# Two layers of a decoder on one core: weight rounding moved among the last queries, and the order of the last head's vector work changed

## The chip, the cores and the metric

The kernel runs on one core of a Trainium2 chip. Its time is the device time of one execution, in microseconds (us). The engines are TensorE (PE, matrix products; its weight loads are listed apart as PEld), VectorE (DVE), ScalarE (ACT), GpSimd (POOL) and SyncE (SP), which issues the transfers from memory. Each engine runs its own list of instructions strictly in the order in which it was written, and waits for the others by semaphores.

## The reference, cut to what matters

The program computes four transformer-like layers for one sequence of 512 positions and width 1024 in float32: retention, latent attention, a short convolution mixer with its feed-forward layer, and differential attention with a second feed-forward layer. The change touches only the differential attention:

```python
k, v = shared_kv(x, g_kv, w_kv)
def diff_attention(h, k, v, dist_bias, w_q, lam_vecs, subln_g, w_o, lambda_init):
    q = (h @ w_q).reshape(b, nb, Q_BLOCK, N_HEADS, 2, HEAD_DIM).transpose(1, 0, 2, 3, 4, 5)
    lam = jnp.exp(jnp.sum(lv[0] * lv[1])) - jnp.exp(jnp.sum(lv[2] * lv[3])) + lambda_init
    def block(args):
        ...
        logits = jnp.einsum('bqhmd,bkhmd->bhmqk', qb.astype(jnp.float32), kf) * scale
        logits = logits + bias[None, :, None]
        ...
        probs = jax.nn.softmax(logits, axis=-1)
        attn = probs[:, :, 0] - lam * probs[:, :, 1]
        return jnp.einsum('bhqk,bkhe->bqhe', attn, vf)
    ...
    o = rms_norm(o, subln_g) * (1.0 - lambda_init)
    return o.reshape(b, s, V_WIDTH).astype(h.dtype) @ w_o
```

There are 8 heads. Each has two maps of scores (p = 0 and 1), which are softmaxed apart and then combined with the factor lambda. Queries come in four groups of 128 rows, i = 0 to 3; group i needs keys 0 to 128(i+1) only.

## The kernel before, in words

**Numbers in two parts.** Every float32 product is made of three products of rounded numbers (high by high, high by low, low by high). So each tensor that PE reads exists as a high part, rounded by ACT, and a low part, the difference, made by DVE or POOL.

**Weights.** The weights stream through in units of 8 blocks of 128x128, 512 KB each, in exactly the order in which PE uses them. SP loads a unit into one of 3 places of `stage`; ACT rounds it into `WH` (L795, `hi_to`), DVE subtracts it into `WL` (L804, `lo_to`), both rings of 4 units. A call `hi_to(act, b)` or `lo_to(dve, b)` does all units up to the one of block b plus 2 (`AHEAD`) that have not been done. PE waits for `w_lo` of a unit before its first product. The units that matter here:

- 209 and 210: queries of heads 6 and 7; 211: keys of head 0; 212 and 213: values of heads 0 and 1, the first and the second four steps of the sum; 214 and 215: keys of heads 1 and 2.
- 227: steps (0, 0) to (5, 0), (0, 1) and (0, 2) of the output projection, in the order of the table below; 228, 229 and 230 are the next ones.

```python
DIF_OUT = {
    "head 7, a": [(0, 0), (1, 0)],
    ...
    "head 7, c": [(4, 0)],
    "head 7, d": [(5, 0)],
    "turn": [(k, m) for k in range(2) for m in (1, 2, 3)],
    "values": [(k, m) for k in (2, 3, 4) for m in (1, 2, 3)],
```

**Start of the attention.** PE makes query(6), query(7), key(0) and the first half of value(0). Behind it DVE scales each query (L2920), ACT rounds it (L2791) and POOL makes its low part (L3102). A key goes the same way: DVE L2930, ACT L2804, POOL L3089. Only after POOL has made the low part of key 0 can PE begin the scores of head 0 (L2675). The order of this work on each engine is the order in which `act_dif`, `dve_dif`, `pool_dif` and `pe_dif` are written.

**A head.** For each group of rows PE makes both maps of scores (L2675) into two of three PSUM banks that are used in turn; DVE adds the bias and takes the maximum (L2949, listed as ISA or CUSTOM_DVE, which frees the bank); ACT takes the exponential (L2816). Then DVE combines the two maps of two groups at a time, `combine(h, 0)` for groups 0 and 1 and `combine(h, 2)` for groups 2 and 3: a reciprocal (L2959), the weight (L2963), two sums (L2969). PE transposes (L2688), ACT (L2823) and DVE (L2975) split the result (`turn`), PE multiplies by the values (`values`), and ACT squares (L2831). PE sums the squares (L2710, `sums_of`) into a bank of the three; DVE reads it (L2988) and takes the root in seven small instructions (L948 to L960); PE spreads it (L2720), ACT copies (L2839), DVE multiplies (L3001, `finish`), ACT and POOL split (L2844, L3095, `rounded`). `sums_of`, `finish` and `rounded` of head h run during heads h+1 and h+2.

**The last head.** Instead of a next key and value, PE has pieces of the output projection between the groups: a, scores of group 1, finish(5), b, scores of group 2, c, scores of group 3, values(6), d (which needs `rounded(5)`), turn of groups 0 and 1, sums_of(6), then the 6 steps "turn". Of these, the products for column 2 go into the bank that sums_of(6) used, so PE waits there until DVE has read the sums (L2988).

Of the kernel before, what the change touches and what calls it, by code (L numbers as in the profile page):

```python
# [15 lines left out]
KD = 8  # L16
# [229 lines left out]
BLOCK = {b: i for i, b in enumerate(ORDER) if b is not None}  # L246
# [64 lines left out]
class Net:  # L311
# [2470 lines left out]
    def act_dif(self, act):  # L2782
        QZ = self.dif_qz

        def key_input(k):
            act.activation(self.dif_xkv(0, k), self.xt(k), ACT.Copy, scale=self.col("g_kv_2", k)).then_inc(
                *self.tick("xg_hi", ("xkv_hi", k)))

        def query(h):
            act.wait_ge(*self.at("q_in", h))  # L2790
            act.activation(QZ[:, 1024 * h:1024 * h + 512], self.place["t", "dif", "q", h], ACT.Copy).then_inc(  # L2791
                *self.tick("q_hi", ("q_hi", h)))

        def key(h):
            if h >= 3:
                rounded(h - 3)
            if h % 2 == 0:
                self.hi_to(act, BLOCK["w_kv_2", KD - 1, h])
                if h:
                    self.hi_to(act, BLOCK["w_kv_2", 3, 9 + h])  # L2800
            act.wait_ge(*self.at("dif_kin", h))
            if h >= 2:
                act.wait_ge(*self.at("pe", "dif", "s", h - 2, 3, 1))
            act.activation(self.dif_k[h % 2][:, 0:512], self.place["t", "dif", "k", h], ACT.Copy).then_inc(  # L2804
                *self.tick("k_hi", ("k_hi", h)))
# [20 lines left out]
        def values(h):  # L2826
            t = ("t", "dif", "osq", "h", h)
            act.wait_ge(*self.at("pe", "dif", "pv", h))
            for w in self.freed(*t):
                act.wait_ge(*w)  # L2830
            act.activation(self.place[t], self.place["dif", "pv", h], ACT.Square).then_inc(  # L2831
                *self.tick("o_sq", ("o_sq", h)))
# [14 lines left out]
        def out(steps):  # L2847
            self.hi_to(act, BLOCK["w_o_2", steps[-1][0], steps[-1][1]])
# [9 lines left out]
        for k in range(4, KD):  # L2858
            key_input(k)
        query(6)  # L2860
        query(7)
        key(0)
        self.hi_to(act, BLOCK["w_kv_2", KD - 1, 9])
        value(0, [0])
        for h in range(8):
            scores(h, 0)
            if h:
                turn(h - 1, 3)
            scores(h, 1)
            if h >= 2:  # L2870
                finish(h - 2)
            scores(h, 2)
            if h < 7:
                key(h + 1)
            else:
                out(DIF_OUT["head 7, c"])
                rounded(5)
            scores(h, 3)
            if h:
                values(h - 1)  # L2880
            if h < 7:
                c = (h + 1) // 2
                turn(h, 0)
                turn(h, 1)
                value(c, [(h + 1) % 2])
                turn(h, 2)
                self.hi_to(act, BLOCK["w_kv_2", KD - 1, 9 + 2 * c if h % 2 else h + 1])
            else:
                out(DIF_OUT["turn"])
                turn(h, 0)  # L2890
                turn(h, 1)
# [13 lines left out]
    def dve_dif(self, dve):  # L2905
# [8 lines left out]
        def query(h):  # L2914
            t, b = ("t", "dif", "q", h), ("dif", "w", h) if h < 6 else ("dif", "q", h)
            dve.wait_ge(*self.at("pe", *b))
            dve.wait_ge(*self.at("r", "dif", "pre"))
            for w in self.freed(*t):
                dve.wait_ge(*w)
            dve.tensor_tensor(self.place[t], self.place[b], R, ALU.mult).then_inc(  # L2920
                *self.tick("q_in", ("q_in", h), ("free", *b)))

        def key(h):
            if h % 2 == 0:
                self.lo_to(dve, BLOCK["w_kv_2", KD - 1, h])
            t, b = ("t", "dif", "k", h), ("dif", "k", h)
            dve.wait_ge(*self.at("pe", *b))
            for w in self.freed(*t):
                dve.wait_ge(*w)
            dve.tensor_tensor(self.place[t], self.place[b], R, ALU.mult).then_inc(  # L2930
                *self.tick("dif_kin", ("dif_kin", h), ("free", *b)))
# [4 lines left out]
        def scores(h, i):  # L2936
            n = 128 * (i + 1)
            if i == 0:
                for p in range(2):
                    self.small(("ds", h, p), 4)  # L2940
                dve.wait_ge(*self.at("bias_table"))
            mx = self.small(("dmx", h, i), 2)
            for p in range(2):
                b = ("dif", "s", h, i, p)
                dve.wait_ge(*self.at("pe", *b))
                if p == 0 or i >= 2:
                    for w in self.freed(*self.dif_row(h, i, p)):
                        dve.wait_ge(*w)
                dve.tensor_tensor_reduce(self.dif_s(h, i, p), self.place[b][:, 0:n], TB[:, h, 512 - n:512], -0.125,  # L2949
                                         3.0e38, ALU.add, ALU.min, mx[:, p:p + 1]).then_inc(  # L2950
                    *self.tick("biased", ("biased", h, i, p), ("free", *b)))

        def combine(h, a):


            w, pair = self.small(("dw", h), 4), slice(a, a + 2)
            s0, s1 = [self.small(("ds", h, p), 4) for p in range(2)]
            dve.wait_ge(*self.at("exp", "dif", h, a + 1, 1))
            dve.reciprocal(w[:, pair], s1[:, pair]).then_inc(*self.tick("row_rec", ("row_rec", "dif", h, a)))  # L2959
            dve.wait_ge(*self.at("row_rec", "dif", h, a))  # L2960
            if (h, a) == (0, 0):
                dve.wait_ge(*self.at("lam"))
            dve.scalar_tensor_tensor(out=w[:, pair], in0=s0[:, pair], scalar=self.lam, in1=w[:, pair], op0=ALU.mult,  # L2963
                                     op1=ALU.mult).then_inc(*self.tick("row_rec", ("weight", h, a)))
            dve.wait_ge(*self.at("weight", h, a))
            for i in (a, a + 1):
                t0, t1 = [self.dif_s(h, i, p) for p in range(2)]
                done = [("free", *self.dif_row(h, i, 1))] if i >= 2 else []
                dve.scalar_tensor_tensor(out=t0, in0=t1, scalar=w[:, i:i + 1], in1=t0, op0=ALU.mult,  # L2969
                                         op1=ALU.add).then_inc(*self.tick("probs", ("probs", "dif", h, i), *done))  # L2970
# [23 lines left out]
        def finish(h):  # L2994
            t, b = ("t", "dif", "t", h), ("dif", "pv", h)
            dve.wait_ge(*self.at("head_r", h))
            if h == 0:
                dve.wait_ge(*self.at("sub_gain"))
            for w in self.freed(*t):
                dve.wait_ge(*w)  # L3000
            dve.scalar_tensor_tensor(out=self.place[t], in0=self.place[b], scalar=self.gs,  # L3001
                                     in1=self.place["t", "dif", "r", h], op0=ALU.mult, op1=ALU.mult).then_inc(
                *self.tick("head_out", ("head_out", h), ("free", *b)))

        def out(steps):
            self.lo_to(dve, BLOCK["w_o_2", steps[-1][0], steps[-1][1]])
# [23 lines left out]
        for k in range(4, KD):  # L3030
            key_input(k)
        query(6)
        query(7)
        key(0)
        self.lo_to(dve, BLOCK["w_kv_2", KD - 1, 9])
        value(0, [0])
        for h in range(8):
            scores(h, 0)
            if h >= 2:
                sums_of(h - 2)  # L3040
            if h:
                turn(h - 1, 3)
            if h % 2:
                self.lo_to(dve, BLOCK["w_kv_2", KD - 1, h])
            scores(h, 1)
            combine(h, 0)
            if h >= 2:
                finish(h - 2)
            scores(h, 2)
            if h < 7:  # L3050
                key(h + 1)
            else:
                out(DIF_OUT["head 7, c"])
            scores(h, 3)
            c = (h + 1) // 2
            if h % 2 and h < 7:
                self.lo_to(dve, BLOCK["w_kv_2", 3, 9 + 2 * c])
            combine(h, 2)
            floor_of(h)
            if h < 7:  # L3060
                turn(h, 0)
                turn(h, 1)
                value(c, [(h + 1) % 2])
                turn(h, 2)
                if h % 2:
                    self.lo_to(dve, BLOCK["w_kv_2", KD - 1, 9 + 2 * c])
            else:
                out(DIF_OUT["turn"])
                turn(h, 0)
                turn(h, 1)  # L3070
# [300 lines left out]
```

## Time and profile before

| What | us |
|---|---|
| Median of 3 runs | 2036.31 |
| Lowest and highest of them | 2034.36, 2037.73 |
| The profiled execution's own time | 2038.49 |
| Span of the profiled execution | 2036.70 |
| PE busy in that span | 1973.4 |
| DVE, ACT, POOL busy | 1253.0, 833.8, 320.7 |
| Mean granted clock of PE, share of full | 0.986 |

A kernel in which PE is busy 97% of the span loses time only where PE stands still, or where its clock is granted at half. All times below are from the start of the span. The differential attention lasts from about 1349 to 1599 us, its last head from 1525 to 1561 us.

### The profile page before, as it was taken

To read this page: it belongs to the slowest core of one execution; us is meant where nothing else is said; L and a number is where in the kernel's file an instruction comes from. 1 tells how busy PE (TensorE), PEld (TensorE's weight loads), DVE (VectorE), ACT (ScalarE), POOL (GpSimd) and SP (SyncE) were. 2 spreads that over 40 slices of the span, in tenths; PEclk is the share of its full clock that TensorE was granted. 3 is DMA by queue.
4 is the path that set the end of the run, shared out by engine and by line. 5 is a ranking of instruction groups with operands and counts; after the bars stand their busy time and mean duration, and the time that the engine had idled before them with its cause. 6 is when DMAs were issued, how large, how long until landed. Compare 5 with 4: busy or idle time off the path is not lost.

```text
span 2036.7 us, 27328 instructions
## 1 busy us (share of the span) xinstructions
PE 1973.4 (97%) x10578; PEld 1692.0 (83%) x10578; DVE 1253.0 (62%) x2219; ACT 833.8 (41%) x1389; POOL 320.7 (16%) x256
## 2 busy tenths in 40 slices
PE   7999999999889999999999999999999999999997
PEld 6889888887778887898888888988887988888896
DVE  6666666267555474457877623786763778775256
ACT  4333333244365443244444423554554444443243
POOL 3332242101132200110111110112111011110101
PEclk9999999999889999999999999999998999999998
DMA  4222222322111224232232422223112323233321
GB/s 156 99 82 88 94 78 73 104 83 95 63 32 32 85 94 129 79 103 93 93 103 85 128 88 93 84 86 112 55 42 63 93 83 99 89 112 114 97 71 62
DMA packets 54824, 179.03 MB, mean 88 GB/s; under 512 B 6279, under 2 KB 10887, under 8 KB 54696
## 3 DMA queue, kind: packets, MB, share of 16 engines
q1 hardware_dynamic: 54696, 177.29, 27.0%
q8 instruction: 84, 1.38, 0.3%
q14 instruction: 44, 0.36, 0.1%
HBM read 172.55 MB, written 4.72 MB: 87 GB/s over the span
## 4 chain that ended last, share of the span: by engine, by line
PE 66%; DVE 5%; ACT 2%; issue 2%; POOL 1%; DVEq 0%; ACTq 0%; POOLq 0%
PE pb L821 62%; DVE WL L804 1%; PE pb L2675 1%; PE pb L921 1%; ACT WH L795 1%; PE pb L2204 0%; PE pb L905 0%; DVE X L1002 0%; PE pb L1719 0%; DVE FD L993 0%; DVE T L2949 0%; PE pb L2720 0%; DVE FR L2910 0%; PE pb L909 0%; POOL FR L2115 0%
## 5 line engine op out<-in xcount | busy, mean ns | idle before, releaser
L821 PE MATMUL pb<-FR,WH 128*128 128x512 f32 (+1 forms) x5100 | 1455.3, 371 | 21.2 <-DVE WL L804 11.4
L821 PEld LDWEIGHTS pb<-FR,WH 128*128 128x128 f32 x5100 | 920.4, 190 | 183.0 <-DVE WL L804 11.4
L821 PE MATMUL pb<-FR,WL 128*128 128x512 f32 (+1 forms) x2550 | 939.6, 368 | 0.0
L804 DVE TENSOR_TENSOR WL<-stage,WH 128x1024 fp32r<-128x1024 f32 x311 | 402.1, 1310 | 407.0 <-ACT WH L795 405.8
L821 PEld LDWEIGHTS pb<-FR,WL 128*128 128x128 f32 x2550 | 484.2, 190 | 80.8
L795 ACT ACTIVATE WH<-stage 128x1024 fp32r<-128x1024 f32 x311 | 319.7, 1051 | 116.8 <-PE pb L821 107.3
L821 PE MATMUL pb<-WH,FR 128*128 128x256 f32 x832 | 156.4, 285 | 2.9 <-DVE T L1306 1.5
L821 PE MATMUL pb<-FR 128*128 128x256 f32 (+3 forms) x752 | 126.1, 319 | 14.0 <-POOL FR L2115 10.0
L821 PEld LDWEIGHTS pb<-FR 128*128 128x128 f32 x752 | 114.1, 198 | 28.4 <-POOL FR L2115 11.1
L821 PEld LDWEIGHTS pb<-WH,FR 128*128 128x128 f32 x832 | 132.0, 192 | 4.5 <-DVE WL L804 2.0
L1285 POOL TENSOR_TENSOR acc<-acc,T 128x512 f32<-128x512 f32 (+1 forms) x53 | 63.7, 1203 | 418.0 <-ACT T L1256 274.9
L821 PE MATMUL pb<-WL,FR 128*128 128x256 f32 x416 | 117.8, 283 | 0.0
L1012 ACT ACTIVATE FR<-X,cols 128x256 fp32r<-128x256 f32 (+1 forms) x88 | 52.2, 605 | 96.9 <-DVE X L1002 96.9
L2428 POOL TENSOR_TENSOR FR<-FD,FR 128x512 fp32r<-128x512 f32 x26 | 33.7, 1297 | 312.7 <-ACT FR L2358 312.7
L821 PEld LDWEIGHTS pb<-WL,FR 128*128 128x128 f32 x416 | 79.9, 192 | 0.1
L1256 ACT ACTIVATE T<-pb 128x512 f32<-128x512 f32 (+1 forms) x51 | 27.3, 535 | 106.0 <-PE pb L821 106.0
L2184 ACT ACTIVATE FD<-FD,cols 128x512 f32<-128x512 f32 x42 | 29.5, 721 | 81.4 <-DVE FD L2389 52.0
L1044 DVE SCALAR_TENSOR_TENSOR FR<-X,cols,FR 128x256 fp32r<-128x256 f32 (+1 forms) x88 | 52.6, 608 | 9.3 <-ACT FR L1012 9.2
L1610 POOL TENSOR_TENSOR FR<-T,FR 128x512 fp32r<-128x512 f32 (+3 forms) x32 | 31.1, 1003 | 158.5 <-ACT FR L1445 158.5
L993 DVE SCALAR_TENSOR_TENSOR T<-FD,cols,pb 128x256 f32<-128x256 f32 x112 | 50.2, 474 | 6.6 <-PE pb L921 6.6
L883 ACT ACTIVATE FR<-pb,held 128x256 fp32r<-128x256 f32 x64 | 26.9, 472 | 64.3 <-PE pb L821 64.0
L892 DVE SCALAR_TENSOR_TENSOR FR<-pb,held,FR 128x256 fp32r<-128x256 f32 x64 | 27.9, 478 | 35.1 <-ACT FR L883 34.9
(227 smaller groups left out, 1673.9 us busy)
## 6 DMA issues: line engine op xcount, KB each, us to landing
stage<-in_ws SPq DMA_DIRECT2D x311, 512.0 KB, 3.6
X<-in_xT SPq DMA_DIRECT2D x8, 256.0 KB, 5.8
FD<-in_decay SPq DMA_DIRECT2D x8, 256.0 KB, 3.8
FD<-scr SPq DMA_DIRECT2D x1, 2048.0 KB, 8.8
out_dram<-X SPq DMA_DIRECT2D x16, 128.0 KB, 1.7
scr<-FD SPq DMA_DIRECT2D x10, 160.0 KB, 5.3
FD<-in_rope_b SPq DMA_DIRECT2D x2, 512.0 KB, 3.5
FD<-in_pT SPq DMA_DIRECT2D x4, 256.0 KB, 5.3
```

What stands on the lines that cost most here:

```text
L795: act.activation(hi, src, ACT.Copy).then_inc(*self.tick("w_hi", ("w_hi", u)))
L804: dve.tensor_tensor(lo, src, hi.bitcast(F32), ALU.subtract).then_inc(*self.tick("w_lo", ("w_lo", u)))
L821: m = pe.matmul(out, l, r, start=first and i == 0, stop=last and i == n - 1)
L892: i = dve.scalar_tensor_tensor(out=lo, in0=src, scalar=self.hold(y)[:, t:t + 1], in1=hi.bitcast(F32), op0=ALU.mult, op1=ALU.subtract)
L993: dve.scalar_tensor_tensor(out=part(t, p), in0=part(self.Y[k], p), scalar=self.col(name, base + k), in1=part(self.place["spread", *key], p ...
L1012: act.activation(part(self.xin(at)(0, k), p), part(self.xt(k), p), ACT.Copy, scale=self.col(name, base + k)).then_inc(*self.tick("xg_hi", ...
L1044: dve.scalar_tensor_tensor(out=part(xin(1, k), p), in0=part(self.xt(k), p), scalar=self.col(name, base + k), in1=part(xin(0, k), p).bitcas ...
L1256: act.activation(part(self.place["t", s, "osq", m], p), b, ACT.Square).then_inc(*self.tick("osq", ("osq", s, m, *q)))
L1285: pool.tensor_tensor(acc, acc, part(self.place["t", s, "osq", m], p), ALU.add).then_inc(*self.tick("acc", *done))
L1610: pool.tensor_tensor(S[:, 1280 + o:1280 + o + n], self.place["t", "ret", "s", h, j][:, 0:n], S[:, o:o + n].bitcast(F32), ALU.subtract).the ...
L2184: act.activation(self.place[o], self.place[u], ACT.Copy, scale=w).then_inc(*self.tick("tap", done))
L2428: pool.tensor_tensor(self.ffn_in(s, 1, m), self.place[t], self.ffn_in(s, 0, m).bitcast(F32), ALU.subtract).then_inc(*self.tick("m_lo", ("f ...
```

## The change: what it does

No instruction is added or removed on any engine, and PE's, POOL's and SP's lists stay as they are. ACT's and DVE's are reordered in two places.

```diff
@@ act_dif
         query(6)
+        self.hi_to(act, BLOCK["w_kv_2", KD - 1, 0])
         query(7)
+        self.hi_to(act, BLOCK["w_kv_2", KD - 1, 9])
         key(0)
-        self.hi_to(act, BLOCK["w_kv_2", KD - 1, 9])
         value(0, [0])
...
             if h < 7:
                 key(h + 1)
             else:
-                out(DIF_OUT["head 7, c"])
                 rounded(5)
             scores(h, 3)
             if h:
                 values(h - 1)
+            if h == 7:
+                out(DIF_OUT["head 7, c"])
@@ dve_dif
         query(6)
+        self.lo_to(dve, BLOCK["w_kv_2", KD - 1, 0])
         query(7)
+        self.lo_to(dve, BLOCK["w_kv_2", KD - 1, 9])
         key(0)
-        self.lo_to(dve, BLOCK["w_kv_2", KD - 1, 9])
         value(0, [0])
...
             scores(h, 1)
-            combine(h, 0)
-            if h >= 2:
+            if h < 7:
+                combine(h, 0)
+                if h >= 2:
+                    finish(h - 2)
+                scores(h, 2)
+                key(h + 1)
+                scores(h, 3)
+            else:
+                scores(h, 2)
                 finish(h - 2)
-            scores(h, 2)
-            if h < 7:
-                key(h + 1)
-            else:
+                combine(h, 0)
+                scores(h, 3)
                 out(DIF_OUT["head 7, c"])
-            scores(h, 3)
```

The two engines' lists show it. In the queries, DVE before: FD<-pb,R are the queries 6 and 7, L804 the weight units, R<-pb,R is key 0, and the last row is the first half of the values.

```order
L2910 SCALAR_TENSOR_TENSOR FR<-X,cols,FR 128x512 x4
L2920 TENSOR_TENSOR FD<-pb,R 128x512 x2
L804 TENSOR_TENSOR WL<-stage,WH 128x1024
L2930 TENSOR_TENSOR R<-pb,R 128x512
L804 TENSOR_TENSOR WL<-stage,WH 128x1024 x2
L892 SCALAR_TENSOR_TENSOR FR<-pb,held,FR 128x256 x2
```

and DVE with the change, where each line from 2910 on has a number higher by 2:

```order
L2912 SCALAR_TENSOR_TENSOR FR<-X,cols,FR 128x512 x4
L2922 TENSOR_TENSOR FD<-pb,R 128x512
L804 TENSOR_TENSOR WL<-stage,WH 128x1024
L2922 TENSOR_TENSOR FD<-pb,R 128x512
L804 TENSOR_TENSOR WL<-stage,WH 128x1024 x2
L2932 TENSOR_TENSOR R<-pb,R 128x512
```

Unit 213 has moved ahead of query 7, and units 214 and 215 have moved ahead of key 0.

The same place on ACT, as a difference; L2791 rounds queries, L2804 key 0, L795 weight units, L883 the values.

```order
-L2791 ACTIVATE FR<-FD 128x512 x2
-L795 ACTIVATE WH<-stage 128x1024
+L2791 ACTIVATE FR<-FD 128x512
+L795 ACTIVATE WH<-stage 128x1024
+L2791 ACTIVATE FR<-FD 128x512
+L795 ACTIVATE WH<-stage 128x1024 x2
 L2804 ACTIVATE FR<-R 128x512
-L795 ACTIVATE WH<-stage 128x1024 x2
 L883 ACTIVATE FR<-pb,held 128x256 x2
```

ACT has moved in step with DVE: key 0 is now behind both later units here too.

In the last head, DVE before, from the scores of group 2 back to the combination of groups 0 and 1 (L2959 to L2969), with finish(5) at L3001, unit 229 at L804 and the scores of group 3 at 128x512:

```order
L2959 RECIPROCAL sm<-sm 128x2
L2963 SCALAR_TENSOR_TENSOR sm<-sm,keep 128x2
L2969 SCALAR_TENSOR_TENSOR T<-T,sm 128x128
L2969 SCALAR_TENSOR_TENSOR T<-T,sm 128x256
L3001 SCALAR_TENSOR_TENSOR acc<-pb,keep,R 128x512
L2949 ISA FD,sm<-pb,FD 128x384
L2949 ISA sm 128x1
L2949 ISA FD,sm<-pb,FD 128x384
L2949 ISA sm 128x1
L804 TENSOR_TENSOR WL<-stage,WH 128x1024
L2949 ISA T,sm<-pb,FD 128x512
```

and with the change:

```order
L2951 ISA FD,sm<-pb,FD 128x384
L2951 ISA sm 128x1
L2951 ISA FD,sm<-pb,FD 128x384
L2951 ISA sm 128x1
L3003 SCALAR_TENSOR_TENSOR acc<-pb,keep,R 128x512
L2961 RECIPROCAL sm<-sm 128x2
L2965 SCALAR_TENSOR_TENSOR sm<-sm,keep 128x2
L2971 SCALAR_TENSOR_TENSOR T<-T,sm 128x128
L2971 SCALAR_TENSOR_TENSOR T<-T,sm 128x256
L2951 ISA T,sm<-pb,FD 128x512
```

The scores of group 2 now come first, then finish(5), then the combination, and unit 229 follows the scores of group 3. On ACT unit 229 has moved from behind the exponentials of group 2 to behind the squares of head 6 (L2831), next to unit 230.

## Rows read from the trace of the kernel before

**Rows 1.** The page: busy time by engine, and the chain that ended last, by engine.

```profile
PE 1973.4 (97%) x10578; PEld 1692.0 (83%) x10578; DVE 1253.0 (62%) x2219; ACT 833.8 (41%) x1389; POOL 320.7 (16%) x256
...
PE 66%; DVE 5%; ACT 2%; issue 2%; POOL 1%; DVEq 0%; ACTq 0%; POOLq 0%
```

**Rows 2.** Chain of waits, 1380 to 1400 us: start, length, what.

```profile
1386.17 4.58 PE pb L821 x36
```

**Rows 3.** Timeline of PE: start, length, what, [idle before <- releaser].

```profile
1386.17 0.39 PE L821 MATMUL pb<-WH,FR 128*128 128x256 f32 x1 [1.05 <-DVE WL L804]
...
1390.68 0.55 PE L2675 MATMUL pb<-FR 64*128 64x128 f32 x6
```

**Rows 4.** Timeline of DVE, queries to values.

```profile
1383.99 2.13 DVE L804 TENSOR_TENSOR WL<-stage,WH 128x1024 fp32r<-128x1024 f32 x1 [1.65 <-ACT WH L795]
1386.04 0.68 DVE L2930 TENSOR_TENSOR R<-pb,R 128x512 f32<-128x512 f32 x1
1388.37 2.61 DVE L804 TENSOR_TENSOR WL<-stage,WH 128x1024 fp32r<-128x1024 f32 x2 [1.65 <-ACT WH L795]
```

**Rows 5.** Timeline of ACT, same stretch.

```profile
1381.78 1.23 ACT L2791 ACTIVATE FR<-FD 128x512 fp32r<-128x512 f32 x2 [5.25 <-DVE FD L2920]
1382.91 1.05 ACT L795 ACTIVATE WH<-stage 128x1024 fp32r<-128x1024 f32 x1
...
1387.29 1.99 ACT L795 ACTIVATE WH<-stage 128x1024 fp32r<-128x1024 f32 x2
```

**Rows 6.** Timeline of POOL, same stretch.

```profile
1382.49 2.55 POOL L3102 TENSOR_TENSOR FR<-FD,FR 128x512 fp32r<-128x512 f32 x2 [3.21 <-ACT FR L2791]
1387.46 1.29 POOL L3089 TENSOR_TENSOR FR<-R,FR 128x512 fp32r<-128x512 f32 x1 [2.43 <-ACT FR L2804]
```

**Rows 7.** Timeline of PE, last head.

```profile
1515.76 2.12 PE L821 MATMUL pb<-FR 128*128 128x512 f32 x12
...
1530.66 0.79 PE L2675 MATMUL pb<-FR 64*128 64x384 f32 x6
...
1534.25 0.97 PE L2675 MATMUL pb<-FR 64*128 64x512 f32 x6 [1.91 <-DVE sm L2949]
1535.15 3.65 PE L821 MATMUL pb<-FR 128*128 128x512 f32 x12
...
1541.44 1.45 PE L2710 MATMUL pb<-ones,T 128*128 128x1 f32 x8 [0.82 <-ACT T L2831]
```

**Rows 8.** Chain of waits, last head.

```profile
1544.54 5.66 PE pb L821 x15
...
1562.05 3.57 PE pb L821 x15
```

**Rows 9.** Timeline of DVE, last head.

```profile
1531.77 0.17 DVE L2959 RECIPROCAL sm<-sm 128x2 f32<-128x2 f32 x1 [1.16 <-ACT T L2816]
...
1532.89 0.74 DVE L3001 SCALAR_TENSOR_TENSOR acc<-pb,keep,R 128x512 f32<-128x512 f32 x1
1533.55 0.54 DVE L2949 CUSTOM_DVE_ANT_0 FD<-pb,FD 128x384 f32<-128x384 f32 x1
...
1536.90 1.23 DVE L804 TENSOR_TENSOR WL<-stage,WH 128x1024 fp32r<-128x1024 f32 x1 [2.32 <-ACT WH L795]
...
1540.94 0.17 DVE L2959 RECIPROCAL sm<-sm 128x2 f32<-128x2 f32 x1 [1.59 <-ACT T L2816]
...
1542.67 1.22 DVE L804 TENSOR_TENSOR WL<-stage,WH 128x1024 fp32r<-128x1024 f32 x1
```

**Rows 10.** Timeline of ACT, last head.

```profile
1539.39 0.72 ACT L2816 ACTIVATE T<-T,sm 128x512 f32<-128x512 f32 x1 [1.99 <-DVE sm L2949]
...
1540.81 0.57 ACT L2831 ACTIVATE T<-pb 128x512 f32<-128x512 f32 x1
```

**Rows 11.** Stretches: us, busy (count) of PE, PEld, DVE, ACT, POOL; granted clock; DMA.

```profile
1384.00:1386.00 2.00, 1.13 (x10) 0.92 (x8) 2.00 (x1) 0.00 (x0) 1.03 (x1) 1.00 0.52 200
...
1546.00:1548.00 2.00, 2.00 (x6) 1.61 (x5) 0.00 (x0) 0.00 (x0) 0.00 (x0) 0.50 0.36 145
```

## Prediction

> **What bounds the kernel now.** I first read the busy times and the chain that ended last. PE is busy for 1973.4 of 2036.70 us, and the chain runs through PE for two thirds of the span [rows 1]. The change gives PE no work and takes none away, so only PE's standing time and its clock can change. The largest possible gain is what PE loses at the two places.
>
> The first place is in the queries. In the timeline of PE the reader is to see one stop: at 1386.17 the second half of value(0) had waited 1.05 us for the low part of unit 213, so PE wanted it at 1385.12. The scores of head 0 follow at 1390.68, without a stop [rows 3]. In the chain of waits PE's 36 products lead up to them, to 1386.17 + 4.58 = 1390.75 [rows 2]: key 0 was ready before. How long before: DVE scales key 0 at 1386.04 [rows 4], and POOL's low part ends at 1387.46 + 1.29 = 1388.75 [rows 6]. That is 2.71 us for the key's way through DVE, ACT and POOL, and it leaves a slack of 1390.68 - 1388.75 = 1.93 us. This slack is what the change draws on.
>
> The second place is the last head. PE stops three times: 1.91 us for a bank that DVE frees with the scores of group 2, 0.82 us for ACT's squares [rows 7], and, in the chain, the restart at 1544.54 for column 2 of the steps "turn" [rows 8], where it has waited for DVE to read the sums of head 6.
>
> **The change, first place.** ACT rounds queries 6 and 7 in 1382.91 - 1381.78 = 1.13 us from start to start, 0.57 each, and then unit 213; DVE starts on that 1383.99 - 1382.91 = 1.08 us later [rows 4, 5]. With unit 213 behind query 6 alone, ACT starts it at 1382.34 and DVE at 1383.42. DVE's subtraction of a unit takes 1.22 us where POOL is idle [rows 9]. Here it took 2.13 [rows 4], beside POOL's two query parts, which ran to 1382.49 + 2.55 = 1385.04 [rows 6]. POOL will by then have only the part of query 6, to about 1383.77, so I charge 0.35 us of standing still: the low part is ready at 1383.42 + 1.22 + 0.35 = 1385.0. PE wants it at 1385.12. The stop of 1.05 us goes, and value(0) ends at 1390.68 - 1.05 = 1389.63.
>
> But key 0 now comes after units 214 and 215. Step by step: DVE scales query 7 from 1385.0 to 1385.6 (0.6, as key 0 of the same size, 0.68 with its overlap [rows 4]); ACT rounds it to 1386.2; ACT rounds unit 214 to about 1387.25, half of its pair of 1.99 plus the handover [rows 5], and unit 215 a microsecond later, ahead of DVE. The slot of unit 215 is free, since PE is through with key 0 before value(0). DVE subtracts both in 2.61 [rows 4], from 1387.25 to 1389.8, again with some 0.3 us beside POOL (now query 7's part, then key 0's). Then key 0 needs its 2.71: 1392.5. PE, which could have gone on at 1389.63, stands for 2.9 us, and the scores of head 0 start 1392.5 - 1390.68 = 1.8 us later than now. All that is queued behind them on PE (key 1, the other groups, the second half of value 0) comes later by as much; DVE and ACT wait for those scores in turn, so nothing ahead of them can catch up. Bounds: if POOL does not hold up DVE and key 0 follows at once, 1.3; if DVE is held up through both units, at the pace of unit 213, 2.61 becomes up to 4.3, and the loss 3.5, but that needs POOL to be busy all the while, and it has one part of 1.3 us to do. I take 1.8 and 1.3 to 2.3.
>
> The Trainium skill, "SBUF — State Buffer", section "Who interferes with whom", says that a DVE instruction with two SBUF inputs and a GpSimd instruction that reads SBUF exclude each other, and that the first to start has the port for its whole length. By that rule unit 213 in the changed kernel waits for the end of query 6's part and then takes 1.22, the same 1385.0; were the rule untrue, it would be ready at 1384.65, which changes nothing, since PE does not want it sooner.
>
> **The clock behind the new stop.** In the last head a stop of 1.91 us was followed by twelve products of values(6) in 3.65 us, where those of values(5) took 2.12 [rows 7]: 1.5 us lost. The stop of 1.05 us in the queries left the granted clock at 1.00 [rows 11]. The new stop of 2.9 us is longer than the one that cost 1.5, so I take 1.5 for it. Behind it, PE is the engine that the chain follows [rows 2], so the loss is on the path. Bounds: nothing if the clock stays, and 2.1, which is what fifteen products lost at half clock, 5.66 against 3.57 us [rows 8]. The two levels here are 2.4 and 1.2 GHz: a stretch inside those fifteen shows 0.50 [rows 11].
>
> **The change, second place.** PE's scores of group 2 start at 1530.66 [rows 7] and DVE can read them some 0.8 us later, at 1531.5, when they are written (0.79). It reads them now only at 1533.55, behind the combination and finish(5) [rows 9]. Moved ahead, both maps are done at about 1532.5 and the first bank is free at 1532.0 (0.54 us for a map, and they overlap a little [rows 9]). PE's stop of 1.91 us goes: it starts group 3 at 1534.25 - 1.91 = 1532.34.
>
> That is not yet a gain at the end, since PE meets DVE again at the restart of 1544.54. DVE goes on: finish(5) 1532.5 to 1533.15 (0.66, from 1532.89 to 1533.55), the combination to 1534.3 (1.12, from 1531.77 to 1532.89), and the scores of group 3 to 1535.5 (1.2 for two of 128x512). ACT takes the exponentials to 1536.95 (1540.81 - 1539.39 = 1.42) and the squares of head 6 to 1537.45 [rows 9, 10]. Only then does it round unit 229, for 1.04, and DVE, which had to wait 2.32 us for this unit before [rows 9], waits again, now until 1538.5. It subtracts to 1539.65, and the second combination follows at once; it started at 1540.94 before [rows 9]. So it is 1.3 us earlier, not 1.9: the unit that moved behind the squares on ACT has taken the rest. From the combination to PE's restart 1544.54 - 1540.94 = 3.6 us go by, all on DVE (the combination, unit 230, two turns, the reading of the sums), and none of it changes. PE restarts at 1543.25: 1.3 us of gain. Bounds: 0.6, if ACT's squares or unit 229 come later than I have them, and 1.9, the whole stop.
>
> PE will have done its earlier pieces sooner and then stands for some 4 us ahead of that restart. It now loses 2.1 us there to the half clock [rows 8]; it will do so again. I take no difference, with 1.3 either way.
>
> **The sum.** 1.8 + 1.5 - 1.3 = +2.0 us, against the profiled execution's own 2038.49 (its span of 2036.70 and 1.79 around it), that is 2040.5. This execution was 2.18 above the median of the runs, 2036.31; against the median the sum gives 2038.3.
>
> **Rivals.**
> - *No clock loss behind the first stop.* What speaks for it: the clock was kept over 1.05 us [rows 11]. Against it: the longer stop. The sum is +0.5: 2036.8. The Trainium skill, "TensorE: Matmul & The Clock Gate", section "What's actually happening", says that the intervals in which the chip watches PE run freely and are not tied to the kernel's start. By that rule the same stop costs more or less from one execution to the next; no rows of one execution can show this.
> - *The half clock lasts: slower.* If it holds behind the new stop for twice as long as it did over values(6), it costs 2 x 1.5 = 3.0 [rows 7], and with 1.8 and -1.3 the sum is +3.5: 2039.8. From a clock term of 4.07 - 0.5 = 3.6 us on, the change is slower by more than 0.2%: 2040.4 and more. For it: the new stop is the longest in this part, and head 0 at half pace may make new stops, each of which feeds the next. Against it: 3.6 us is more than any row shows; the longest, over fifteen products, is 2.1 [rows 8].
> - *The gain side.* The key's delay does not reach PE (DVE would have to be done with both units by 1387 instead of 1389.8), so that the first place gives its 1.05, and the second gives 1.3 and keeps its full clock, another 2.1: -4.45, 2031.9. Against it: [rows 4] have the duration of the pair, and a stop of 4 us stands ahead of that restart.
> - *The last head gives nothing.* PE only moves its waiting, and DVE's wait for unit 229 grows by as much as the scores were advanced: 0 there, +3.3 in all: 2039.6.
>
> **How the numbers follow.** 0.2% is 4.07 us, about what a measurement can tell from no change. My forecast, +1 to +3, has 0.46; without clock loss, -1 to +1, 0.22; the last head without gain, 0.14, all three within 0.2%, as are half of the lasting half clock (0.12 in all) and some of the gain side (0.06). This makes 0.86 within, 0.09 slower and 0.05 faster. The range for 8 in 10 reaches from -1.5 (both places with their good bounds, no clock loss) to +4.3: 2034.8 to 2040.6.
>
> **What would show it.** In the changed profile: PE runs through unit 213 near 1385 without a stop; a new stop of 2.5 to 3.3 us ahead of the scores of head 0, ended by POOL's L3096 (the key's low part, L3089 now); the granted clock at 0.5 for a stretch behind it; DVE's L804 twice ahead of L2932. In the last head, counted from its first scores: no stop ahead of the scores of group 3, a stop of about 4 us ahead of column 2 that DVE ends, and DVE's wait for unit 229 ahead of the second combination. I am wrong if DVE subtracts units 214 and 215 much faster than in 2.61, if PE's delay at head 0 is taken up by slack in head 0, or if the half clock falls elsewhere than where I have it.

## The result, and the profile after

| | before | changed |
|---|---|---|
| Median of 10 executions each, us | 2036.97 | 2042.62 |
| Lowest and highest | 2034.36, 2039.80 | 2039.54, 2044.93 |
| Span of the profiled execution | 2036.70 | 2043.1 |
| Mean granted clock of PE in it | 0.986 | 0.985 |

The ratio is 1.0023, with an interval of 1.0015 to 1.0031. The changed kernel is slower, by 5.65 us between the medians. The forecast was 2038.3 with a range of 2034.8 to 2040.6: the result lies outside, on the side of slower. Two executions of this study, one of the kernel before (2778.84 us) and one of "key 0 first" below (3261.65 us), ran at a mean granted clock of 0.654 and 0.555 and are left out of every median here.

The page of the changed kernel: span, busy time by engine, and the chain that ended last, by engine.

```profile
span 2043.1 us, 27328 instructions
...
PE 1974.8 (97%) x10578; PEld 1692.8 (83%) x10578; DVE 1252.9 (61%) x2219; ACT 833.7 (41%) x1389; POOL 320.2 (16%) x256
...
PE 67%; DVE 5%; ACT 2%; issue 2%; POOL 1%; DVEq 0%; ACTq 0%; POOLq 0%
```

Both executions with a trace are slower than their medians: the one of the kernel before took 2038.49 us, 1.5 above, and the one of the changed kernel 2044.93, 2.3 above and the slowest of its ten. So the traces below explain a difference of 6.4, and not the 5.65 of the medians.

Against [rows 1] PE's busy time has risen by 1.4 us and the span by 6.4. The page does not say where; the timelines do. DVE of the changed kernel in the queries comes first. Each line has the start, the length, what runs, and the idle time before it with its releaser.

```profile
1386.52 1.47 DVE L804 TENSOR_TENSOR WL<-stage,WH 128x1024 fp32r<-128x1024 f32 x1 [1.65 <-ACT WH L795]
1387.91 0.68 DVE L2922 TENSOR_TENSOR FD<-pb,R 128x512 f32<-128x512 f32 x1
1390.23 2.62 DVE L804 TENSOR_TENSOR WL<-stage,WH 128x1024 fp32r<-128x1024 f32 x2 [1.65 <-ACT WH L795]
1392.77 0.68 DVE L2932 TENSOR_TENSOR R<-pb,R 128x512 f32<-128x512 f32 x1
```

Unit 213 takes 1.47 us now, where it took 2.13 beside POOL's two query parts [rows 4]. The pair 214 and 215 takes 2.62, as before, and key 0 is scaled only behind it. The chain of waits of the changed kernel through head 0:

```profile
1374.80 17.82 PE pb L821 x101
1392.62 2.94 issue
1395.56 0.90 PE pb L2675 x6
...
1407.14 3.06 PE pb L821 x24
```

In 101 products there is no stop, so the 1.05 us of [rows 3] are gone. Then PE stands for 2.94 us ahead of the scores of head 0; the profile shows no releaser for it ("issue"). What ended it is in POOL's timeline: the low part of key 0 is done at 1394.19 + 1.27 = 1395.46, 0.1 us before the scores start.

```profile
1394.19 1.27 POOL L3096 TENSOR_TENSOR FR<-R,FR 128x512 fp32r<-128x512 f32 x1 [3.56 <-ACT FR L2804]
```

And behind the stop, the granted clock (the column ahead of the last two) of two stretches of the changed kernel:

```profile
1396.00:1401.00 5.00, 5.00 (x20) 3.53 (x19) 1.22 (x8) 0.88 (x4) 0.00 (x0) 0.50 0.04 16
...
1402.00:1406.00 4.00, 4.00 (x21) 2.76 (x19) 2.18 (x8) 1.12 (x5) 0.00 (x0) 1.00 0.02 4
```

The clock was at its lower level, 1.2 GHz, for at least the five microseconds shown, 20 product records, and at full from 1402 on. In the last head the changed kernel has this, DVE first, then PE:

```profile
1546.01 1.23 DVE L804 TENSOR_TENSOR WL<-stage,WH 128x1024 fp32r<-128x1024 f32 x1 [3.02 <-ACT WH L795]
1547.16 0.16 DVE L2961 RECIPROCAL sm<-sm 128x2 f32<-128x2 f32 x1
```

```profile
1539.75 0.96 PE L2675 MATMUL pb<-FR 64*128 64x512 f32 x6
1540.82 2.10 PE L821 MATMUL pb<-FR 128*128 128x512 f32 x12
...
1550.75 1.22 PE L821 MATMUL pb<-FR,WH 128*128 128x512 f32 x2 [3.79 <-DVE sm L2990]
```

The stop of 1.91 us ahead of the scores of group 3 [rows 7] is gone, and the twelve products behind them run in 2.10 instead of 3.65. DVE waits 3.02 us for unit 229 instead of 2.32 [rows 9], and PE 3.79 us for DVE's reading of the sums.

To compare executions that begin a few microseconds apart, I cut the way of PE into pieces with fixed ends: M, the start of the six scaled queries 0 to 5 on DVE (L2920, listed as x6; L2922 in the changed kernel), which lies ahead of all that the change moves; S, the first scores of head 0; V, the second half of value 0 (the call behind the scores of head 0, 24 products in the chain; not the second four steps, ahead of which the forecast has its first stop); H, the first sums of squares of the last head (sums_of(5)); R, PE's restart for column 2; Q, the transposes behind its fifteen products. All are differences of two starts in one trace.

| profiled execution | start to M | M to S | S to V | V to H | H to R | R to Q |
|---|---|---|---|---|---|---|
| before | 1368.78 | 21.90 | 9.01 | 124.47 | 20.38 | 5.65 |
| changed | 1371.91 | 23.65 | 11.58 | 124.49 | 19.12 | 5.85 |
| difference | +3.13 | +1.75 | +2.57 | +0.02 | -1.26 | +0.20 |

These add up to the +6.4 of the span; behind Q nothing differs. Of it, 3.13 us are earlier than anything that the change touches, so only +3.3 can be the change. Of the 3.13, 1.88 are lost at the very start of the program. PE's first product, first in the kernel before, then in the changed one:

```profile
11.45 1.22 PE L821 MATMUL pb<-FR,WH 128*128 128x512 f32 x2 [11.45 <-DVE WL L804]
```

```profile
13.33 1.22 PE L821 MATMUL pb<-FR,WH 128*128 128x512 f32 x2 [13.33 <-DVE WL L804]
```

In the other eleven traces, the repeat of the changed kernel among them, this product starts between 11.13 and 11.81.

### The profile page after: what moved, and what is told of

It reads as the page before. It is cut to its first block, busy times and chain, and to the rows that moved or that the text cites. A ratio compares the mean times of both kernels' runs of the same rounds, so it can differ in the third digit from the quotient of the medians.

```text
span 2043.1 us, 27328 instructions
## 1 busy us (share of the span) xinstructions
PE 1974.8 (97%) x10578; PEld 1692.8 (83%) x10578; DVE 1252.9 (61%) x2219; ACT 833.7 (41%) x1389; POOL 320.2 (16%) x256
## 4 chain that ended last, share of the span: by engine, by line
PE 67%; DVE 5%; ACT 2%; issue 2%; POOL 1%; DVEq 0%; ACTq 0%; POOLq 0%
PE pb L821 63%; PE pb L2675 1%; PE pb L921 1%; DVE WL L804 1%; ACT WH L795 1%; PE pb L2204 0%; PE pb L905 0%; DVE X L1002 0%; PE pb L2720 0%; PE pb L1719 0%; DVE FD L993 0%; DVE T L2951 0%; PE pb L909 0%; POOL FR L2115 0%; POOL acc L1285 0%
## 5 line engine op out<-in xcount | busy, mean ns | idle before, releaser
L804 DVE TENSOR_TENSOR WL<-stage,WH 128x1024 fp32r<-128x1024 f32 x311 | 401.6, 1309 | 407.5 <-ACT WH L795 406.2
L795 ACT ACTIVATE WH<-stage 128x1024 fp32r<-128x1024 f32 x311 | 319.6, 1051 | 117.3 <-PE pb L821 104.7
L883 ACT ACTIVATE FR<-pb,held 128x256 fp32r<-128x256 f32 x64 | 26.9, 472 | 62.7 <-PE pb L821 62.5
```

The costliest lines, as they stand in the source:

```text
L795: act.activation(hi, src, ACT.Copy).then_inc(*self.tick("w_hi", ("w_hi", u)))
L804: dve.tensor_tensor(lo, src, hi.bitcast(F32), ALU.subtract).then_inc(*self.tick("w_lo", ("w_lo", u)))
```

## The experiments

The kernels were measured in three sets, each with the kernel before (medians 2037.32, 2037.48 and 2037.39). Differences below are of the medians, against the kernel before in the same set, and the interval is that of the ratio. Each ratio is uncertain by about 0.0009, or 1.8 us. The pieces of a trace are known far better, but they are those of one execution, so I use both.

**The queries alone.** The queries as changed, the last head as before (DVE's part of the edit to the changed kernel; ACT's puts unit 229 back ahead of `rounded(5)`).

```diff
             scores(h, 1)
+            combine(h, 0)
+            if h >= 2:
+                finish(h - 2)
+            scores(h, 2)
             if h < 7:
-                combine(h, 0)
-                if h >= 2:
-                    finish(h - 2)
-                scores(h, 2)
                 key(h + 1)
-                scores(h, 3)
             else:
-                scores(h, 2)
-                finish(h - 2)
-                combine(h, 0)
-                scores(h, 3)
                 out(DIF_OUT["head 7, c"])
+            scores(h, 3)
```

> The new order in the queries alone; the last head as before. Theory A (key 0 behind units 214 and 215 delays PE, and the stop halves the clock): PE stands 2.9 us ahead of the scores of head 0, 1.75 later than before counted from the first query's scaling, and head 0 then loses 2.6 to half clock over 6.8 us: +4.3 us in all. Rival B (the slower time comes from outside the two places, for example the 3.1 us that the changed kernel's profile lost in its first 60 us): the times show +4 and more only together with such a late start, and a run without it is +1.8 or less. Rival C (it is the last head that costs): 0.

Measured: 2040.81, +3.5 us, 1.0019 (1.0010 to 1.0028). Expected were +4.3. The trace has the same stop and the same delay, but a smaller loss in head 0:

```profile
1388.49 2.93 issue
1391.42 0.55 PE pb L2675 x6
...
1401.73 3.08 PE pb L821 x24
```

S to V is 10.31 us, 1.30 more than before. The queries' new order carries the loss by itself: it is as slow as the changed kernel in its repeat below.

This kernel's last head is that of the kernel before, and it shows something about the row from which the forecast took its price of 1.5 us. PE there:

```profile
1536.32 0.96 PE L2675 MATMUL pb<-FR 64*128 64x512 f32 x6 [1.91 <-DVE sm L2950]
1537.22 2.12 PE L821 MATMUL pb<-FR 128*128 128x512 f32 x12
```

Behind the same stop of 1.91 us the twelve products take 2.12 us and not the 3.65 of [rows 7]. It is so in the two other kernels with that last head, "key 0 first" (2.14 behind 1.89) and "one unit ahead of key 0" (2.14 behind 1.90).

**The last head alone.** The queries as before.

```diff
         query(6)
-        self.lo_to(dve, BLOCK["w_kv_2", KD - 1, 0])
         query(7)
-        self.lo_to(dve, BLOCK["w_kv_2", KD - 1, 9])
         key(0)
+        self.lo_to(dve, BLOCK["w_kv_2", KD - 1, 9])
```

(and the same on ACT)

> The new order in the last head alone; the queries as before. Theory A: -1.1 to -1.3 us, DVE's second combination 1.3 us earlier and PE's restart for column 2 with it, a stop of about 4 us ahead of it, half clock behind it as before. Rival C (the last head costs, since its longer stop holds the clock down longer): +1 to +3.

Measured: 2036.70, -0.6 us, 0.9997 (0.9988 to 1.0006). H to R is 19.11 us, 1.27 less than before, so the gain is there in the trace; in the time it is smaller than what can be told. The two parts add up to 3.5 - 0.6 = +2.9.

**Key 0 first.** On top of the queries alone: unit 213 stays ahead of query 7, key 0 goes ahead of units 214 and 215 (here and below, ACT's calls move with DVE's).

```diff
         self.lo_to(dve, BLOCK["w_kv_2", KD - 1, 0])
         query(7)
-        self.lo_to(dve, BLOCK["w_kv_2", KD - 1, 9])
         key(0)
+        self.lo_to(dve, BLOCK["w_kv_2", KD - 1, 9])
```

> Only unit 213 is moved ahead of query 7; key 0 stays ahead of units 214 and 215, and the last head is as before. Theory A (all the cost of the queries hangs on the order of key 0 and units 214 and 215): unit 213 is ready when PE wants it, key 0 is ready before PE has done the first half of value 0, no stop and full clock: -1.0 us. Rival B: as slow as the changed kernel, +3 or more, if any difference of order moves the start. Rival D (POOL's parts of query 7 and key 0 hold up unit 214, which PE wants for key 1): a stop of 0.5 to 1 us ahead of key 1, sum 0.

Measured: 2036.07, -1.3 us, 0.9994 (0.9985 to 1.0003), which can't be told from no change. M to S is 20.64 us, 1.26 less than before: in the trace the gain from unit 213 is there. S to V gives 0.43 of it back. The pair of units stands ahead of the first half of the values and of the first maps on DVE, as it did before, and it ends 22.2 us behind M in both kernels: it starts sooner now, but takes 3.27 us instead of 2.61, with POOL's part of key 0 beside it for 1.1 us instead of 0.4. So DVE comes to the scores' maxima later than PE's earlier scores would let it, and PE waits 0.52 us for it. DVE and PE of this kernel:

```profile
1388.69 3.27 DVE L804 TENSOR_TENSOR WL<-stage,WH 128x1024 fp32r<-128x1024 f32 x2 [1.65 <-ACT WH L795]
```

```profile
1393.10 0.61 PE L2675 MATMUL pb<-FR 64*128 64x256 f32 x6 [0.52 <-DVE sm L2950]
```

**The stop filled.** This separates the stop from the clock: the changed kernel, with twelve products whose result is never used, into the bank of the first scores, while PE would stand.

```diff
         value(0, [0])
+        for w in self.freed("dif", "s", 0, 0, 0):
+            pe.wait_ge(*w)
+        for i in range(12):
+            pe.matmul(self.place["dif", "s", 0, 0, 0], self.dif_xkv(0, 0)[:, 0:128], self.dif_xkv(0, 1), start=True, stop=True)
         for h in range(8):
```

> The changed kernel with twelve products of 128x512 more on PE between the first half of value 0 and the scores of head 0, into the bank that the scores then overwrite; their result is used nowhere. They take 2.7 of the 2.9 us for which PE stands there. Theory A (the stop costs 1.75 by delay and 2.6 by half clock): the delay stays, the clock stays at 1.00 through head 0, and it is 2.6 us faster than the changed kernel, +3 against before in the mean of runs. Rival E (head 0 is slow by its waits and not by the clock): no faster than the changed kernel, or slower by what the products add.

Measured: 2037.75, +0.4 us, 1.0001 (0.9992 to 1.0011). The chain of waits and the clock of this kernel:

```profile
1388.04 2.75 PE pb L2746 x12
1390.78 0.22 issue
1391.00 0.55 PE pb L2675 x6
...
1399.84 3.08 PE pb L821 x24
```

```profile
1391.00:1400.00 9.00, 9.00 (x50) 6.28 (x51) 4.36 (x19) 3.57 (x13) 0.00 (x0) 1.00 0.10 39
```

The scores come as late as in the changed kernel (M to S 23.66 against 23.65), but the clock is at full from S to V, and that piece is 8.84 us. The times agree: +0.4 is 2.6 less than the repeat of the changed kernel below, though not the +3 that was expected. So the loss in head 0 is the clock's, and not that of DVE or ACT running late behind the delayed key: those have the same delay here.

**The changed kernel again**, to see whether the first measurement repeats. No edit.

> The changed kernel once more, since the first measurement, +4.9 us in the mean of ten runs, is 2.0 more than the two parts measured alone (+3.5 and -0.7). If the parts add up: +2.9. If they do something to each other: +4.9 again, and then its last head or head 0 takes longer in the trace than in the kernels with one part alone.

Measured: 2040.52, +3.0 us, 1.0013 (1.0004 to 1.0022), 11 executions. The chain, and the clock over the nine microseconds behind the stop:

```profile
1387.62 2.94 issue
1390.56 0.55 PE pb L2675 x6
...
1400.88 3.08 PE pb L821 x24
```

```profile
1391.00:1400.00 9.00, 9.00 (x40) 6.13 (x38) 3.37 (x16) 3.09 (x11) 0.00 (x0) 0.81 0.04 16
```

The same program, with the same stop of 2.94 us, lost 1.31 us in head 0 here and 2.57 in the first profile; and M is at 1366.91 instead of 1371.91. Both differences belong to the execution and not to the order. The intervals of the two measurements overlap (from 1.0015 and up to 1.0022). The execution with a trace is the slowest of ten in the first and the fastest of eleven in the second. The mean granted clock of each execution, listed with its time, goes along: in the first measurement 6 of 10 executions of the changed kernel had 0.985 (mean 2043.2 us), in the second 2 of 11 (2042.3), and most had 0.986 (2040.5).

**One unit ahead of key 0.** The queries alone, with unit 214 ahead of key 0 and 215 behind it.

```diff
         query(7)
-        self.lo_to(dve, BLOCK["w_kv_2", KD - 1, 9])
+        self.lo_to(dve, BLOCK["w_kv_2", 3, 9])
         key(0)
+        self.lo_to(dve, BLOCK["w_kv_2", KD - 1, 9])
```

> The queries with unit 213 ahead of query 7 and unit 214 alone ahead of key 0; unit 215 behind key 0 as before; the last head as before. Theory A (each unit ahead of key 0 delays it by its own 1.3 us): key 0 is 1.3 us earlier than with both units, PE stands about 1.6 us instead of 2.9 and the scores of head 0 start 0.5 us later than before, counted from the first query's scaling; by times 0 to +1.5 us against before, depending on whether the clock is halved behind a stop of that length. Rival: as slow as with both units, +3.5.

Measured: 2038.40, +1.0 us, 1.0009 (1.0000 to 1.0018). PE of this kernel:

```profile
1389.55 0.55 PE L2675 MATMUL pb<-FR 64*128 64x128 f32 x6 [1.81 <-issue]
```

M to S is 20.64, 22.53 and 23.65 us with none, one and two units ahead of key 0. So the first unit costs 1.89 and the second 1.12. The stop of 1.81 us is already followed by the half clock: the two products behind head 0's first scores take 1.22 us, where they take 0.73 at full clock, and S to V is 10.38.

**The changed kernel with key 0 first.**

```diff
         query(7)
-        self.lo_to(dve, BLOCK["w_kv_2", KD - 1, 9])
         key(0)
+        self.lo_to(dve, BLOCK["w_kv_2", KD - 1, 9])
```

> The changed kernel, but with key 0 back ahead of units 214 and 215 on ACT and DVE; unit 213 stays ahead of query 7, the last head as changed. Theory A: -1.3 for the queries and -0.7 for the last head: -2.0 us against before. If the order of key 0 were not the cause: +3 or more, as the changed kernel.

Measured: 2034.61, -2.9 us, 0.9985 (0.9976 to 0.9993). Moving two units back behind one key turns the changed kernel from 3.0 us slower into 2.9 us faster.

**The unit early on ACT.** The queries as before; the last head on DVE as changed, on ACT as before, with unit 229 behind the exponentials of group 2.

```diff
             else:
+                out(DIF_OUT["head 7, c"])
                 rounded(5)
             ...
-            if h == 7:
-                out(DIF_OUT["head 7, c"])
```

> Queries as before; DVE's last head as changed; ACT rounds unit 229 where it did before, behind the exponentials of group 2. Theory F (the changed last head gains little because DVE waits 3.0 us for unit 229, which ACT rounds only behind the squares): DVE subtracts unit 229 while ACT takes the exponentials of group 3, the second combination starts some 2.6 us earlier than in the changed kernel and PE's restart with it: -4 us against before, and up to 2 more where the shorter stop keeps the clock. Rival G (POOL's part of head 5 comes 1 us later, behind unit 229 on ACT, and PE waits for that): -1 to -2.

Measured: 2035.47, -2.0 us, 0.9986 (0.9977 to 0.9995). DVE and PE of this kernel, last head:

```profile
1535.77 2.33 DVE L804 TENSOR_TENSOR WL<-stage,WH 128x1024 fp32r<-128x1024 f32 x1
```

```profile
1537.07 0.74 PE L821 MATMUL pb<-FR,WH 128*128 128x512 f32 x2 [1.29 <-POOL FR L3099]
...
1541.61 1.22 PE L821 MATMUL pb<-FR,WH 128*128 128x512 f32 x2 [0.85 <-DVE sm L2988]
```

Expected were -4; the time lies at the rival's -1 to -2, whose reason, POOL's part of head 5, is in the trace. DVE no longer waits for ACT; H to R is 17.12 us, another 2.0 less than in the changed kernel. The wait of 3.02 us has not become a gain of 3.02: the subtraction takes 2.33 us instead of 1.23. What stands beside it is POOL's low part (L3099), for which PE waits 1.29 us. POOL's part runs from 1535.75 for 1.27 us, and DVE's subtraction, begun at 1535.77, takes 1.10 longer. It is the same lengthening as in [rows 4], 2.13 beside POOL against 1.22 without, and it agrees with the rule of "SBUF — State Buffer" that the forecast cited from the Trainium skill.

**Both.** Key 0 first in the queries, the unit early in the last head.

> Key 0 ahead of units 214 and 215 with unit 213 ahead of query 7, and the last head of early_unit. If the two places are independent: the sum of -1.3 and what early_unit gives, -5 to -7 us against before.

Measured: 2031.39, -6.1 us, 0.9969 (0.9957 to 0.9980). This rests on 6 executions. The same kernel a second time, with 11:

> both_best once more, since it was timed only six times: -6 us against before, in half of the executions no half-clock stretch in the differential attention.

Measured: 2032.48, -4.9 us, 0.9974 (0.9966 to 0.9983). H to R is 17.12 and 17.11 us, as with the unit early alone, but R to Q is 3.69 and 3.73 instead of 5.62: the fifteen products run at full clock. It fits with this that both together gain more than the sum of the two alone, -1.3 and -2.0.

**Unit 230 behind the reading of the sums**, on top of both, on DVE alone.

```diff
             else:
-                out(DIF_OUT["turn"])
                 turn(h, 0)
...
         sums_of(6)
+        out(DIF_OUT["turn"])
         turn(7, 2)
```

> both_best, and in the last head DVE subtracts unit 230 only behind the reading of head 6's sums and their root. Theory: the reading comes 1.1 us earlier, PE's stop ahead of column 2 shrinks from 1.7 to about 0.5, -1.1 us against both_best. Rival: PE wants the sums no sooner, or unit 230 is then late for the steps "root": 0 or slower.

Measured: 2030.11, -7.3 us, 0.9968 (0.9956 to 0.9980). PE of this kernel:

```profile
1537.59 0.73 PE L821 MATMUL pb<-FR,WH 128*128 128x512 f32 x2 [0.50 <-DVE sm L2989]
```

H to R is 15.98 us, 1.14 less again, about one subtraction of a unit (1.22). This is the fastest kernel of the study. In the same set "both" had 2032.48: the median is 2.4 lower and the mean 1.9, with 6 executions against 11, and the spans of the two traces differ by 1.4.

## Why the prediction was wrong

By its own steps:

- **The stop at unit 213 goes.** Right: no stop; unit 213 took 1.47 us against 1.22 + 0.35 = 1.57 in the forecast. (The row that the forecast gives for the clock behind the old stop, 1384 to 1386, ends before PE went on at 1386.17; the clock was 1.00 from 1386 to 1390 too.)
- **Key 0 behind two units: a stop of 2.9 us, the scores 1.8 later.** Right: 2.94 and 1.75. The experiments with none, one and two units show that it is the units that do it.
- **The clock behind the new stop, +1.5, at most 2.1.** This is the step that failed: the mechanism was right, the term was sized too small. It took the size from one stop in the last head, twelve products that lost 1.5 us, and the upper end from fifteen that lost 2.1 [rows 7, 8]. Neither row is a price. In three other executions the same twelve products lost nothing behind the same stop, and the half clock of the fifteen had begun ahead of the restart, where their count starts: two products at 1542.75 took 1.20 us, 0.72 in the changed kernel. In the profile of the changed kernel the term was 2.57, outside the bound; in two other executions with the same stop 1.31 and 1.30, within it and close to the 1.5. The kernel with the stop filled takes the clock term away: it is at +0.4 where the changed kernel is at +3.0 in the repeat. By the times that makes the term about 2.6 us, with an uncertainty as large; by the two traces, 10.32 against 8.84 us from S to V, it is 1.5.
- **The last head, -1.3.** Right in size: -1.26 and -1.27, and the stops with it (none ahead of the scores of group 3, 3.79 us ahead of the restart against "about 4"). DVE's wait for unit 229 rose as forecast. That no difference in the clock comes with it held too: R to Q is 5.85 against 5.65. One stop was overlooked: PE stood not three times but four, the fourth for POOL's low part of head 5.

```profile
1539.31 0.74 PE L821 MATMUL pb<-FR,WH 128*128 128x512 f32 x2 [0.52 <-POOL FR L3095]
```

  In the kernel with the queries alone, where the twelve products ahead of it were at full clock, this stop was 2.04, and the product started 15.14 us behind H as against 15.15. So the 1.5 us that the forecast read as lost were taken up here and cost the last head nothing.
- **The sum against the median.** The forecast stood on a median of 3 executions, 2036.31; with 10 it is 2036.97. That is 0.7 of the 4.3 us by which the forecast fell short.

Put together for the profiled execution: 1.75 + 2.57 + 0.02 - 1.26 + 0.20 = +3.3, where the forecast had +2.0; 1.1 of the difference is the clock term. Of the rivals this is the half clock that lasts (+3.5). That rival's mechanism, its place and nearly its price are what this trace shows; the forecast gave it 0.12. But the same pieces of the repeat's trace, 1.75 + 1.31 - 0.01 - 1.26 - 0.17, make +1.6, a little under the forecast. And even +3.3 would lie inside the range, whose upper end was +4.3: the failed step alone does not carry the result out of it. The 3.13 us ahead of M, which the repeat of the same program lacks (M at 1366.91), belong to the profiled execution and not to the order; how many of the other nine had something like them no trace shows. The other rivals fall: the clock loss is there in all three traces with this stop, the last head gains in the trace, and the key's delay does reach PE.

Two sums of the forecast don't come out. The chances that it counts as within 0.2%, 0.46, 0.22, 0.14 and half of 0.12, are 0.88 before anything of the gain side, more than the 0.86 that it gives. And both places with their good bounds and no clock loss make 1.3 - 1.9 = -0.6, not -1.5. Neither bears on the miss.

**What stays open.** The first measurement says +5.65, the repeat +3.0, the parts by themselves +2.9. The traces account for 3.3 at most. The other 2.4 us of the first measurement are not tied to any part of the change. They go with the share of executions at a mean clock of 0.985, and the two intervals overlap; chance in the sampling would do, and so would late starts like that of the profiled execution, but both are argued and not shown. The three later sets ran on three chips, and for the first measurement the chip isn't recorded, so that a difference between chips isn't excluded either. Why the clock costs 2.57 in one execution and 1.31 in another behind the same stop isn't shown either. The Trainium skill, "TensorE: Matmul & The Clock Gate", section "What's actually happening", has the intervals in which the chip watches PE run freely, not tied to the kernel; the forecast cited it for a rival with no loss. That the same order lost 1.31 and 2.57 us agrees with it, and so does the pair of kernels in the last section; neither shows the intervals themselves. The forecast should have made a spread of its clock term out of it, and not only a rival on the good side.

## What to carry to other kernels

Weight preparation that is wanted later must not be moved ahead of an operand that PE waits for next, even where the engine's list looks tidier: here the first unit cost 1.9 us and the second 1.1, and the stop that they made on PE cost another 1.3 to 2.6 in clock. Price a new stop of some 2 to 3 us on a busy PE with a spread and not with one row: here 1.3 to 2.6 us behind the stops in the queries, and anything from nothing to 1.5 behind the stop of 1.9 in the last head. And when a wait is to be shortened, follow it through each engine: in the last head DVE's earlier scores gained 1.3 us alone, 3.3 with the unit left early on ACT, and 4.4 with the next unit taken off DVE's way to the sums.

## What the runs showed of the hardware

The half clock does not follow from the length of one stop. The stop of 1.9 us in the last head, with 3.65 us behind it in one execution and 2.12 to 2.14 in three, is one case. Another is the last head with the unit early on ACT: PE had the same stop of 1.29 us ahead of the same product in two kernels. Behind it two later products show the clock, first with the unit early alone, then with both:

```profile
1539.13 1.20 PE L821 MATMUL pb<-FR,WH 128*128 128x512 f32 x2
```

```profile
1536.46 0.70 PE L821 MATMUL pb<-FR,WH 128*128 128x512 f32 x2
```

The first kernel had lost its clock there, ahead of the restart. That its stop ahead of the restart is the shorter one, 0.85 us against 1.66, comes from this, since PE got there later. The stretch behind the restart of the two, in the same order:

```profile
1541.00:1545.00 4.00, 3.39 (x8) 2.72 (x9) 1.69 (x10) 0.00 (x0) 0.00 (x0) 0.50 0.45 141
```

```profile
1539.00:1543.00 4.00, 3.94 (x19) 3.29 (x20) 1.15 (x8) 0.00 (x0) 0.00 (x0) 1.00 0.46 131
```

Eight product records in four microseconds against nineteen. Behind stops of one length the loss differs too: R to Q is 5.85 us in the changed kernel, behind 3.79, and 5.07 in the changed kernel with key 0 first, behind 3.80, where 3.69 is the time at full clock.

Executions of one and the same kernel differ in mean granted clock, and their time mostly goes with it: the kernel before had in the first set 9 executions at 0.986 with a mean of 2039.1 us, 12 at 0.987 with 2037.3, 7 at 0.988 with 2036.6 and 3 at 0.989 with 2035.3. One more, at 0.953, had 2035.9 us and does not fit. The others make some 1.3 us for each 0.001, so two profiles can lie 3 us apart with no difference in the order at all. And the way to M, all ahead of the change, varied from 1366.91 to 1371.91 us, both of these in the changed kernel.
